# Attention of a two-layer encoder: weighted values by column halves, and softmax inverses spread by a matmul

## What is computed

```python
# mixer A, per head and chunk of 64 queries (band of 576 keys)
sc = einsum('qd,kd->qk', qc, kc) * scale + bias;  p = softmax(sc);  out = p @ vc
# mixer B, grouped heads, window of two chunks, a learned sink per head
m = max(max(sc), sink);  p = exp(sc - m)
p = p / (sum(p) + exp(sink - m));  o = p @ vb
```

## Time and profile before

| | |
|---|---|
| median of 3 runs | 2674.0 us (2669.9 to 2674.36) |
| profiled execution, its own time | 2678.14 us |
| its span, first to last instruction | 2676.2 us |
| mean granted TensorE clock | 0.996 |
| attention stage, layer 0 / layer 1 | 281.5 to 520.1 us / 1603.4 to 1840.2 us |

### The profile page before, as it was taken

The page is one execution under the profiler, slowest core; times in us unless marked ns, Lnnn a source line. Parts: engine busy times, 40 slices in busy tenths (PEclk is TensorE's granted clock), DMA queues, the critical chain, the costliest instruction groups (busy, mean ns, idle before and its releaser), DMA issues. The chain is left out here.

```text
span 2676.2 us, 36725 instructions
## 1 busy us (share of the span) xinstructions
PE 2631.9 (98%) x12920; PEld 2208.2 (83%) x12920; DVE 1923.2 (72%) x3579; ACT 1159.0 (43%) x2429; POOL 252.6 (9%) x390
## 2 busy tenths in 40 slices
PE   8999999999999999999999999999999999999998
PEld 6888888888888888888878888888888888888886
DVE  8766667644787787767996666775448887776687
ACT  6222677732533333344542227775325333333444
POOL 0000311244100000000000011112440000000000
PEclk9999999999999999999999999999999999999999
DMA  4323433253222332385423243332531332234843
GB/s 147 122 104 115 155 102 111 75 183 115 87 99 103 114 118 84 106 269 176 153 99 122 99 144 123 119 97 88 188 120 61 114 110 88 103 114 136 267 124 126
DMA packets 185236, 333.21 MB, mean 125 GB/s; under 512 B 17248, under 2 KB 62688, under 8 KB 185056
## 3 DMA queue, kind: packets, MB, share of 16 engines
q1 hardware_dynamic: 176832, 307.67, 34.6%
q10 hardware_dynamic: 8224, 23.20, 2.6%
HBM read 237.09 MB, written 92.80 MB: 123 GB/s over the span
## 5 line engine op out<-in xcount | busy, mean ns | idle before, releaser
L1203 PE MATMUL ps<-op_hi,up_hi 128*128 128x512 f32 x1232 | 479.9, 390 | 2.5 <-DVE third_sum L2781 2.5
L1205 PE MATMUL ps<-op_hi,up_lo 128*128 128x512 f32 x1232 | 479.3, 389 | 0.0
L1204 PE MATMUL ps<-op_lo,up_hi 128*128 128x512 f32 x1232 | 479.3, 389 | 0.0
L1203 PE MATMUL ps<-in_hi,up_hi 128*128 128x512 f32 x728 | 286.9, 394 | 3.3 <-DVE up_lo L2279 2.1
L1205 PE MATMUL ps<-in_hi,up_lo 128*128 128x512 f32 x728 | 285.0, 392 | 0.0
L1204 PE MATMUL ps<-in_lo,up_hi 128*128 128x512 f32 x728 | 285.0, 392 | 0.0
L1878 ACT ACTIVATE up_hi<-up_raw 128x512 fp32r<-128x512 f32 x252 | 158.0, 630 | 276.9 <-PE ps L1205 271.1
L1203 PEld LDWEIGHTS ps<-op_hi,up_hi 128*128 128x128 f32 x1232 | 231.3, 188 | 51.1 <-issue 3.3
L1205 PEld LDWEIGHTS ps<-op_hi,up_lo 128*128 128x128 f32 x1232 | 231.3, 188 | 48.3
L1204 PEld LDWEIGHTS ps<-op_lo,up_hi 128*128 128x128 f32 x1232 | 231.3, 188 | 47.6
L1173 POOL CAST w_hi<-w_raw 128x256 fp32r<-128x256 f32 x192 | 85.3, 486 | 1757.7 <-DMA w_raw<-w_lin 1199.7
(11 more groups left out here) (266 smaller groups left out, 5406.8 us busy)
## 6 DMA issues: line engine op xcount, KB each, us to landing
up_raw<-w_gu SPq DMA_DIRECT2D x42, 1024.0 KB, 5.1
act_raw<-ff_saved SPq DMA_DIRECT2D x154, 256.0 KB, 2.7
w_quarter<-w_lin SPq DMA_DIRECT2D x52, 512.0 KB, 4.4
w_raw<-w_lin SPq DMA_DIRECT2D x48, 512.0 KB, 3.7
ff_saved<-ff_block SPq DMA_DIRECT2D x88, 256.0 KB, 2.0
ff_saved<-ff_mix SPq DMA_DIRECT2D x66, 256.0 KB, 2.1
gated<-gates_saved SPq DMA_DIRECT2D x32, 512.0 KB, 4.1
stage<-in_saved SPq DMA_DIRECT2D x48, 256.0 KB, 2.8
```

Of the source, the lines that this page charges most:

```text
L1203: pe.matmul(out, w1, x1, start=first, stop=False, skip_group_check=True)
L1204: pe.matmul(out, w1, x0, start=False, stop=False, skip_group_check=True)
L1205: return pe.matmul(out, w0, x1, start=False, stop=last, skip_group_check=True)
```

## The change

In `weigh` the operands change places. The values of one head (64 columns) become the stationary operand, and the turned probabilities (128 columns) are streamed; the result is feature-major, head 0 in PSUM partitions 0 to 63, head 1 in 64 to 127, that is, in the two column halves of the array. Both heads of a pair are done together, in even steps, block by block in turn, and `weigh` now stands ahead of `turn`.

The normalization moves. `spread` takes the two columns of inverses, broadcast over 64 columns, as stationary operand and streams the identity, again one head in each half, so that each inverse stands along its row of tokens in 64 partitions. ACT copies that to `inverse_wide` (`take_wide`), and DVE's `take_heads` multiplies the heads' outputs by it, straight into `x_sb`. `turn_pair`, `take_pair` and `o_tok` are gone, and with them two waits ahead of `turn_values`.

In B both units of a pair are turned in one (odd) step into neighbouring columns, and ACT copies them at once, 256 columns wide; `soft` gives B units two places in each `probs` buffer. `take_heads` moves behind `row_max` of its step. `FILL_A` deals the same number of gate steps (26 in the first A phase, 8 in each later one) to other steps, in later phases to odd ones.

```diff
-FILL_A = ((3, 3, 3, 2, 2, 2, 2, 1, 1, 1, 1, 1, 1, 1, 1, 1), (1, 1, 1, 1, 1, 0, 1, 0, 1, 0, 0, 0, 1, 0, 0, 0))
+FILL_A = ((3, 3, 3, 3, 2, 3, 1, 2, 1, 1, 0, 1, 1, 1, 0, 1), (0, 1, 0, 2, 0, 1, 0, 1, 0, 1, 0, 1, 0, 1, 0, 0))
 FILL_B = (14, 14, 14, 12)
...
     return g * PHASE + r - PHASE + 1
+def groups_turned(u):
+    g, r = divmod(u + 1, UNITS_PER_GROUP)
+    return g * (PHASE + PHASE // 2) + min(r, PHASE) + max(r - PHASE, 0) // 2
+TURN_GROUPS = GROUPS * (PHASE + PHASE // 2)
+HEAD_PAIRS = UNITS // 2
...
-        o_tok = at("o_tok", [P, 2, P], F32, TAB + 14592)
+        inverse_wide = at("inverse_wide", [P, 2, P], F32, TAB + 14592)
...
             return bank(5 if mixer == "B" and u // 2 % 2 else 6)[:, 0:P]
+        def wide_ps(u):
+            mixer, _, _, _ = unit(u)
+            return bank(5 if mixer == "B" and u // 2 % 2 else 6)[:, P:2 * P]
+        def soft(u):
+            mixer, _, _, _ = unit(u)
+            first = u // NPROBS % 2 * P if mixer == "B" else 0
+            return probs[u % NPROBS][:, first:first + (P if mixer == "B" else A_COLS)]
+        def soft_last(u):
+            mixer, _, _, _ = unit(u)
+            return u - (2 * NPROBS if mixer == "B" and u % PHASE >= NPROBS else NPROBS)
         v_ps = bank(7)[:, 0:2 * P]
...
                 pe.wait_ge(softened, L * UNITS + u + 1)
-                if u > 0:
-                    pe.wait_ge(turned_ready, L * UNITS + u)
+                if u > 0 and (mixer == "A" or e == 0):
+                    pe.wait_ge(turned_ready, L * TURN_GROUPS + groups_turned(u - 1))
+                first = e if mixer == "B" else 0
                 for j in range(key_blocks(mixer, p)):
-                    mm = pe.transpose(t_ps[:, j * P:(j + 1) * P], probs[u % NPROBS][:, j * P:(j + 1) * P], ident[:, :])
+                    mm = pe.transpose(t_ps[:, (first + j) * P:(first + j + 1) * P], soft(u)[:, j * P:(j + 1) * P], ident[:, :])
                 mm.then_inc(turned, 1)
             def weigh(L, u):
-                mixer, g, e, p = unit(u)
+                mixer, g, _, p = unit(u)
                 nb = key_blocks(mixer, p)
+                n = L * HEAD_PAIRS + u // 2
                 if mixer == "A":
-                    values = [va[:, p + 1 - nb + j, e * HD:(e + 1) * HD] for j in range(nb)]
-                    if e == 0 and p % 2 == 0:
+                    blocks = [va[:, p + 1 - nb + j, :] for j in range(nb)]
+                    turns = probs_t
+                    if p % 2 == 0:
                         pe.wait_ge(v_ready, L * VALUES + V_PARTS * rank(CONV.index(("va", g, p // 4))) + p % 4 // 2 + 1)
...
                     v, block = (vb, chunk // 2) if chunk % 2 or chunk == 0 else (vb_odd, chunk // 2 - 1)
-                    values = [v[:, block, e * HD:(e + 1) * HD]]
-                    if e == 0 and p == 0:
+                    blocks = [v[:, block, :]]
+                    turns = [probs_t[u // 2 % 2][:, e * P:(e + 1) * P] for e in range(2)]
+                    if p == 0:
                         pe.wait_ge(v_ready, L * VALUES + V_PARTS * (rank(CONV.index(("vb", 0, min(g, 1)))) + 1))
-                    if e == 0 and (g, p) in ((0, 2), (1, 0)):
+                    if (g, p) in ((0, 2), (1, 0)):
                         pe.wait_ge(vb_shifted[g], 32 * (L + 1))
-                pe.wait_ge(turned_ready, L * UNITS + u + 1)
-                n = L * (UNITS // 2) + u // 2
+                pe.wait_ge(turned_ready, L * TURN_GROUPS + groups_turned(u))
                 taken = n - 1 if mixer == "B" and u % PHASE > 1 else n
-                if e == 0 and taken > 0:
+                if taken > 0:
                     pe.wait_ge(head_free, taken)
                 for j in range(nb):
-                    mm = pe.matmul(o_ps(u)[:, e * HD:(e + 1) * HD], probs_t[u % 2][:, j * P:(j + 1) * P], values[j],
-                                   start=(j == 0), stop=(j == nb - 1))
+                    for e in range(2):
+                        rows = slice(e * HD, (e + 1) * HD)
+                        mm = pe.matmul(o_ps(u)[rows, :], blocks[j][:, rows], turns[e][:, j * P:(j + 1) * P],
+                                       start=(j == 0), stop=(j == nb - 1))
                 mm.then_inc(head_done, 1)
-            def turn_pair(L, u):
...
+            def spread(L, u):
+                n = L * HEAD_PAIRS + u // 2
+                pe.wait_ge(inverse_ready, n + 1)
+                for e in range(2):
+                    mm = pe.matmul(wide_ps(u)[e * HD:(e + 1) * HD, :], stat[:, u % NSTAT - 1 + e, 6:7].to_broadcast([P, HD]), ident[:, :],
+                                   start=True, stop=True)
+                mm.then_inc(wide_made, 1)
...
                 pe.wait_ge(in_taken, in_takes(L, IN_PAIRS - 1, 6))
-                for s in range(UNITS + 5):
+                for s in range(UNITS + 3):
                     if s < UNITS:
...
                         gate_step(L, i, k)
-                    if 2 <= s < UNITS + 2:
-                        turn(L, s - 2)
-                    if 3 <= s < UNITS + 3:
+                    weighed = s >= 4 and s % 2 == 0
+                    if weighed:
                         weigh(L, s - 3)
+                    u = s - 2
+                    if 0 <= u < UNITS:
+                        if unit(u)[0] == "A":
+                            turn(L, u)
+                        elif u % 2:
+                            turn(L, u - 1)
+                            turn(L, u)
+                    if weighed:
+                        spread(L, s - 3)
                     for i, k in steps[1:]:
                         gate_step(L, i, k)
-                    if s > 5 and s % 2 == 0:
-                        if values_before(s) > 0:
-                            pe.wait_ge(v_ready, L * VALUES + values_before(s))
-                        turn_pair(L, s - 5)
                     for c, part in turns_at(s):
-                        if s > 6:
-                            pe.wait_ge(pair_ready, L * (UNITS // 2) + (s - 5) // 2)
                         turn_values(L, c, part)
...
                  st = stat[:, u % NSTAT, :]
-                buf = probs[u % NPROBS]
+                buf = soft(u)
                 act.activation(buf[:, c0:c1], buf[:, c0:c1], ACT.Exp, bias=st[:, 0:1], scale=-1.0, accum_out=st[:, 3:4]).then_inc(softened, 1)
...
             def take_turned(L, u):
                 mixer, _, _, p = unit(u)
-                cols = key_blocks(mixer, p) * P
+                cols = key_blocks(mixer, p) * P if mixer == "A" else 2 * P
+                dst = probs_t[u % 2 if mixer == "A" else u // 2 % 2]
                 act.wait_ge(turned, L * UNITS + u + 1)
                 if u >= 2:
-                    act.wait_ge(head_done, L * UNITS + u - 1)
-                act.activation(probs_t[u % 2][:, 0:cols], t_ps[:, 0:cols], ACT.Copy).then_inc(turned_ready, 1)
-            def take_pair(L, u):
...
+            def take_wide(L, u):
+                n = L * HEAD_PAIRS + u // 2
+                act.wait_ge(wide_made, n + 1)
+                if n >= 2:
+                    act.wait_ge(head_free, n - 1)
+                act.activation(inverse_wide[:, n % 2, :], wide_ps(u), ACT.Copy).then_inc(wide_ready, 1)
             def attention(L):
...
                     raise_half(L, c)
-                for s in range(UNITS + 6):
-                    g, r = divmod(s, UNITS_PER_GROUP)
-                    if s > 6 and s % 2 == 1:
-                        take_pair(L, s - 6)
+                for s in range(UNITS + 4):
+                    if s >= 5 and s % 2 == 1:
+                        take_wide(L, s - 4)
                     for c, part in turns_at(s - 1):
                         take_values(L, c, part)
-                    if 2 <= s < UNITS + 2:
+                    if 2 <= s < UNITS + 2 and (unit(s - 2)[0] == "A" or s % 2 == 1):
                         take_turned(L, s - 2)
...
             def split_o(L):
-                act.wait_ge(pair_ready, (L + 1) * (UNITS // 2))
+                act.wait_ge(head_free, (L + 1) * HEAD_PAIRS)
                 for j in range(KT):
...
                 st = stat[:, u % NSTAT, :]
-                buf = probs[u % NPROBS]
+                buf = soft(u)
                 if u >= NPROBS:
-                    dve.wait_ge(turned, L * UNITS + u - NPROBS + 1)
+                    dve.wait_ge(turned, L * UNITS + soft_last(u) + 1)
                 if c1 % P:
...
             def take_heads(L, u):
-                n = L * (UNITS // 2) + u // 2
-                dve.wait_ge(head_done, L * UNITS + u + 1)
-                dve.wait_ge(inverse_ready, n + 1)
-                if u >= 4:
-                    dve.wait_ge(pair_turned, n - 1)
-                inverse = stat[:, u % NSTAT - 1:u % NSTAT + 1, 6:7].to_broadcast([P, 2, HD])
-                dve.tensor_tensor(o_tok[:, n % 2, :].rearrange("p (e d) -> p e d", e=2),
-                                  o_ps(u).rearrange("p (e d) -> p e d", e=2), inverse, ALU.mult).then_inc(head_free, 1)
```

(52 more changed lines are left out.)

4 lines of the change are left out of this document (removed).

## The result

The changed kernel takes 2706.4 us (median of 4 runs, 2705.43 to 2707.01); the kernel before, beside it, 2672.7 (2669.9 to 2674.36). The ratio is 1.0127, 95% interval 1.0109 to 1.0144: slower by 1.3%. The forecast was 2657. The profiled execution of the changed kernel took 2707.0 us of its own time, against 2678.1 before: 28.8 us more.

A forecast was written before the change was run, and what follows sets the result against it. PE was taken to bound the kernel. Terms -37 + 12 + 17 - 4 - 2 - 3 = -17 us took the profiled 2678 to 2661; the median runs 4 lower, so forecast 2657, range 2634 to 2715.

The forecast's parts named there:

- What bounds the kernel: Attention stages: PE is busy nearly throughout, so a us of its work removed is nearly a us of time.
- What goes and what comes: PE's weighing, pair transposes and spread: 143 us removed, 106 us added with halves side by side, a gain of 37.
- the lone instruction at a batch's end: First and last half-width instructions of a batch run alone: 53.5 ns more for each of 256 batches, 14 us.
- The rival of halves taking turns: Half-width weighing and spread on PE do not run side by side: +62 us, 2736; chance 0.15.
- A change of width: PE between full and half width in A and B: 384 changes, 336 paid at 0.05 us, 17 us.
- The first change of width of those pairs: The 48 A pairs of groups 1 to 3: PE's switch to half width costs nothing while it awaits ACT's copy.
- The first rival: PE empties at each boundary between scores, weighing, transposes and spread: 2695 to 2731, deciding from 0.10 us a change; chance 0.26.
- the wait ahead of the weighing: PE waits for ACT's copy of the second head, 0.25 us on each of 48 A pairs: 12 us.
- the waits at the pair transpose: PE's waits there, 1.6 us in layer 0 and 4.5 in the run, go away: 4 us gained.
- ACT's relief: ACT's copies in the stages make it 10 us less busy, worth 3 us where ACT holds PE.
- The end of the stage: Each attention stage ends without a turn of `take_pair` and transpose: 1 us a layer, 2 us gained.

The follow-up runs named there:

- control product: Kernel before, with one more full-width float32 product ahead of the weighing of every first head: 2690.4 us, ratio 1.0064.
- pair of extra products: Kernel before with one more product ahead of every first head's weighing: full width 2690.4 us (1.0064), half width 2714.7 us (1.0159).
- short copy: Changed kernel, ACT copying only the first block of turned probabilities in A: 2696.7 us, 1.0092; same cut in the kernel before: 2672.2 us, 0.9994.

## Why the prediction was wrong

**What bounds the kernel** held. PE sets the time of the stage, and work put into it showed, but not one for one: the control product cost 0.07 us an instruction where 0.106 was expected.

**What goes and what comes**, the term of -37, was right in each factor: 0.054 us for a half-width instruction of 128 columns, two heads side by side, the lone instruction at a batch's end. The rival of halves taking turns is out; it had given 0.107.

**A change of width** is the first step that failed. The forecast took 0.05 us "near that and nearer the lower end, because small and large, float32 and float32r, transposes and products already alternate here with nothing worse". The nearest row was a change of kind, which is another thing: at those PE goes on overlapping its instructions, and at this one it runs nearly empty. Measured it is 0.096 bare, in the changed kernel, and the pair of extra products shows the price with nothing else changed. The sentence "The first change of width of those pairs hides in the wait" held in its mechanism, though for some 40 weighings, in B more than in A, and not for the 48 pairs that it meant. So +17 becomes +33: nearly all of the -37. The first rival named the mechanism and its break-even, 0.10; the trace's value lies just under that point, and under the rival's 0.164, because the next instruction starts 0.07 us before the last one's end. With this price alone put right the forecast's own sum is -1: no change. The loss itself is the next step. The Trainium skill's "TensorEngine Tiling (Array Packing)", Key Properties, was on the right side with its drain at each change of mode. It gives no price. The trace agrees with the rule as far as the 0.07 us before the end.

**The waits** are the second step, and the larger one in us. The forecast's +12 for the wait ahead of the weighing came near the 10 us that the short copy gives back, but by luck. Of its 48 pairs of A twelve are held, for 5 us. "[M]ost B steps have a gate step, 0.7 us, as cover" is so, but the other B steps stood at nothing, and 20 weighings are held there, for 12 us. "[L]ater-group conversions on ACT and DVE have slack" failed where phases begin: two copies a layer come late behind them (7 us), and scores wait for converted keys and queries. What it also had at nothing is what stands in the odd step once the weighing has left it. "SP and POOL keep their work: gate steps are as many ... only dealt to other steps; that costs nothing while PE is full in both kinds of step": PE is not full there. An odd step without a gate step is transposes and scores, and the scores wait for `row_max` (3.1 us in 7 places of layer 0; 10.5 in 20 with the old dealing). The forecast's cover went in the opposite direction, too: -4 for the waits at the pair transpose and -3 for ACT's relief never showed, and waits as large stand at the phase starts now. In place of a net +5 stand 21 us of waits more than before, 6 of lower clock behind the longest of them, and some 11 in small gaps whose cause I leave open.

**The end of the stage**, 2 us in the forecast, can't be read from these runs: outside the stages kernels with the old end differ by as much as the two profiles do.

The forecast's last sentence said that a clock under 1.00 inside the stage would mean that PE was kept waiting far more than it said. That is what the windows show. The sum by the measured terms is -37 + 33 + 21 + 6 + 11 = +34, from 2672.7 to 2707. It closes because the 11 are what is left over; without them it is 2696.

## What to carry to other kernels

Count the changes of array width before the instructions saved: in this kernel two changes cost 0.19 us and a halved small float32 instruction saved 0.05, so the first four of a batch only pay for its changes, and B's weighing has no more than four. Give the half-width work of a step one stretch, and price the change by a pair of runs that differ in nothing but the width of one product.

When a hand-written pipeline takes work out of every second step, look at what each of the two kinds of step is left with; the light one waits for the engines behind it, even where no engine is fuller than before.

## What I had not expected of the hardware

At a change of width PE runs nearly empty: the next instruction starts 0.07 us before the modelled end of the one ahead, where instructions of one width mostly start 0.16 before it. Behind a wait that is longer than this there is nothing left to pay: the half-width weighing then starts as soon after the copy (0.05 us) as scores of unchanged width after DVE's minimum (0.06).

A few waits can cost more by the clock than one of them by itself. In layer 0 a stretch at the lower clock followed waits of 1.4 and 1.9 us and cost 3 us. The same two waits in layer 1 had none behind them.
